# A decoder trunk on one core: the side products of the attention stage moved to other places in the order of work

## What is computed

```python
h = rmsnorm(x, g_attn)
(q_a, kv_cmp, kv_slc, kv_win, gate_a, q_b, k_b, v_b, r_b, lr_b, merge) = split(h @ w_in)
# attention: three branches, each softmax(q k^T - slope * distance) v
kv_c = compress_kv(concat(past_cmp, kv_cmp))         # 16-row blocks, small MLP
o_cmp, p_cmp = cmp_attend(q, kv_c)                   # over the compressed blocks
idx = top-16 blocks by p_cmp                         # 64 rows each
o_slc = sel_attend(q, blocks[idx])                   # over the selected rows
o_win = win_attend(q, last 512 rows)                 # over the recent rows
o_a = ga0 * o_cmp + ga1 * o_slc + ga2 * o_win
# gated linear attention from q_b, k_b, v_b, lr_b; swish gate r_b  -> o_b
mix = sigmoid(merge_a) * (o_a @ w_pa) + sigmoid(merge_b) * (o_b @ w_pb)
x = x + mix @ w_out
x = x + (gelu(causal_dwconv3(h2 @ w_u)) * (h2 @ w_g)) @ w_down,   h2 = rmsnorm(x)
```

## Time and profile before

| | |
|---|---|
| median of 3 runs | 2435.87 us (2433.31 to 2438.61) |
| profiled execution | 2436.56 us, span 2434.8 us |
| PE busy | 2385.6 us (98%), 13063 matmul instructions |
| DVE, ACT, POOL busy | 809.5, 539.0, 104.8 us |
| mean granted clock of PE | 0.986 of 2.4 GHz |
| attention stage, layer 0 | about 100 to 515 us of the span |
| attention stage, layer 1 | about 1306 to 1720 us of the span |

### The profile page before, as it was taken

One profiled execution on the slowest core, in us unless ns is written; L12 is line 12 of the kernel. 1 busy time (PEld: TensorE's weight loads), 2 busy tenths in 40 slices (PEclk: granted clock), 3 DMA queues, 4 the chain that ended last, 5 costly groups with the idle time before them and its releaser, 6 DMA issues.

```text
span 2434.8 us, 30974 instructions
## 1 busy us (share of the span) xinstructions
PE 2385.6 (98%) x13063; PEld 1926.0 (79%) x13063; DVE 809.5 (33%) x1893; ACT 539.0 (22%) x1085; POOL 104.8 (4%) x190
## 2 busy tenths in 40 slices
PE   8999899999999999999999999999999999999999
PEld 7787766678888888888888877667788888888887
DVE  4554545544114222210035544465441232222000
ACT  2353124432011111110013522244220111111000
POOL 4010010001000000000000100000000000000000
PEclk9999999999999999999999999999899999999999
DMA  7553421112222222212373544111122222222222
GB/s 231 186 200 142 197 95 52 32 41 89 70 72 70 70 78 79 66 51 72 77 265 130 219 162 183 53 36 36 49 95 72 69 70 70 70 82 65 63 72 73
DMA packets 186988, 237.55 MB, mean 98 GB/s; under 512 B 38047, under 2 KB 172704, under 8 KB 181984
## 3 DMA queue, kind: packets, MB, share of 16 engines
q1 hardware_dynamic: 175208, 133.11, 18.4%
q0 software_dynamic: 11200, 102.36, 11.1%
q10 hardware_dynamic: 444, 0.12, 0.0%
HBM read 222.76 MB, written 21.11 MB: 100 GB/s over the span
## 4 chain that ended last, share of the span: by engine, by line
PE 93%; DVE 4%; DMA 1%; ACT 1%; issue 1%; SPq 0%; POOL 0%; DVEq 0%; ACTq 0%; POOLq 0%
PE PS L818 52%; PE PS L1441 13%; PE PS L840 6%; PE PS L938 4%; PE PS L866 2%; DVE arena L1810 2%; PE PS L926 2%; PE PS L437 2%; PE PS L1219 2%; PE PS L1208 2%; PE PS L1136 1%; DMA arena<-in_cache_kv_slc_dram,idx 1%; ACT arena L1472 1%; PE PS L1181 1%; PE PS L1147 1%
## 5 line engine op out<-in xcount | busy, mean ns | idle before, releaser
L818 PE MATMUL PS<-hT,ring 128*128 128x272 f32 x4352 | 1010.1, 394 | 2.5 <-DVE small L2254 1.9
L818 PEld LDWEIGHTS PS<-hT,ring 128*128 128x128 f32 x4352 | 827.9, 191 | 175.5 <-issue 8.7
L1472 ACT ACTIVATE arena<-PS 64x512 f32<-64x512 f32 (+13 forms) x467 | 231.3, 518 | 1185.8 <-PE PS L818 559.8
L1441 PE MATMUL PS<-arena,ring 128*128 128x272 f32 x1408 | 323.7, 393 | 0.0
L1441 PEld LDWEIGHTS PS<-arena,ring 128*128 128x128 f32 x1408 | 268.0, 191 | 54.1
L1810 DVE COPY arena<-PS 64x512 f32<-64x512 f32 (+4 forms) x201 | 142.7, 710 | 268.6 <-PE PS L818 98.4
L1801 DVE TENSOR_TENSOR arena<-PS,arena 128x544 f32<-128x544 f32 (+3 forms) x124 | 76.0, 624 | 398.2 <-PE PS L818 380.9
L818 PE MATMUL PS<-arena,ring 128*128 128x272 f32 x768 | 177.2, 393 | 3.1 <-DVE arena L1801 3.1
L818 PEld LDWEIGHTS PS<-arena,ring 128*128 128x128 f32 x768 | 146.2, 191 | 33.5 <-DVE arena L1801 4.0
L1807 DVE SCALAR_TENSOR_TENSOR arena<-arena,prm 128x32 f32<-128x32 f32 (+1 forms) x176 | 88.1, 500 | 249.1 <-ACT arena L1472 245.8
L1801 DVE TENSOR_TENSOR xT<-PS,xT 128x544 f32<-128x544 f32 x32 | 23.2, 724 | 386.3 <-PE PS L1441 303.2
(11 more groups left out here) (309 smaller groups left out, 1665.3 us busy)
## 6 DMA issues: line engine op xcount, KB each, us to landing
ring<-in_w_up_dram SPq DMA_DIRECT2D x88, 512.0 KB, 4.6
ring<-in_w_in_dram SPq DMA_DIRECT2D x68, 512.0 KB, 4.8
ring<-in_w_down_dram SPq DMA_DIRECT2D x32, 384.0 KB, 3.8
ring<-in_w_down_dram SPq DMA_DIRECT2D x32, 320.0 KB, 4.5
arena<-in_state_kv_win_dram POOLq DMA_DIRECT2D x4, 2048.0 KB, 20.4
ring<-in_w_out_dram SPq DMA_DIRECT2D x16, 512.0 KB, 4.1
out_dram<-in_state_kv_win_dram POOLq DMA_DIRECT2D x2, 4064.0 KB, 23.8
ring<-in_w_in_dram SPq DMA_DIRECT2D x16, 256.0 KB, 5.0
```

Source lines behind the costliest of these rows:

```text
L818: mm = pe.matmul(PS[0:m, b + a, 0:HALF], weight(k), rhs(k)[:, HALF * a:HALF * a + HALF], start=(k == 0), stop=(k == nk - 1))
L1441: mm = pe.matmul(PS[:, b + a, 0:HALF], w[:, k, :], aT[:, 11 * half + k, HALF * a:HALF * a + HALF], start=(half == 0 and k == 0), stop=(hal ...
L1472: return nc.scalar.activation(out, in_, func, **kw)
```

## The change

The side products move to other places. No product is added or removed, and no arithmetic changes.

| place | before | after |
|---|---|---|
| behind `hidden(33)`, new ("s",0,5) | none | vb00 |
| ("s",0,4) | vb0l (two tiles) | vb01 |
| ("s",0,3) | qb0 | qb0 |
| ("s",0,2) | qb1 | qb1, kb0 |
| ("s",0,0) | kb0 | kb1 |
| ("b",0) | kb1, vb0b | vb0b, vb0h |
| ("b",1) | vb0h | vb1l |
| ("b",2) | vb1l | vb1h, vb1b |
| ("s",1,0) | vb1h, vb1b | rb00, in pool "S", copied once `os1` is filled |
| ("u",0) | rb00 | rb01 |
| ("u",j) | 11 products at 2,5,8,11,14,17,20,23,25,28,31 | 10 products at 2,5,8,11,14,17,20,23,26,30 |

Besides, `ost` with its wait for `os_ready` moves behind `vbf`, `score(0)` and `score(1)` on PE, and its copies on DVE behind `maxima(0)` and `maxima(1)`. ACT no longer takes `exps(2)` ahead of its copies of unit 0.

```diff
@@ -198,9 +198,9 @@
...
-    at = {("s", 0, 4): ("vb0l",), ("s", 0, 3): ("qb0",), ("s", 0, 2): ("qb1",), ("s", 0, 0): ("kb0",), ("b", 0): ("kb1", "vb0b"),
-          ("b", 1): ("vb0h",), ("b", 2): ("vb1l",), ("s", 1, 0): ("vb1h", "vb1b"), ("u", 0): ("rb00",)}
-    for j, name in zip((2, 5, 8, 11, 14, 17, 20, 23, 25, 28, 31), ["rb01", "rb10", "rb11"] + [f"ga{m}" for m in range(KC)]):
+    at = {("s", 0, 5): ("vb00",), ("s", 0, 4): ("vb01",), ("s", 0, 3): ("qb0",), ("s", 0, 2): ("qb1", "kb0"), ("s", 0, 0): ("kb1",),
+          ("b", 0): ("vb0b", "vb0h"), ("b", 1): ("vb1l",), ("b", 2): ("vb1h", "vb1b"), ("s", 1, 0): ("rb00",), ("u", 0): ("rb01",)}
+    for j, name in zip((2, 5, 8, 11, 14, 17, 20, 23, 26, 30), ["rb10", "rb11"] + [f"ga{m}" for m in range(KC)]):
         at["u", j] = (name,)
@@ -953,6 +953,20 @@
...
+                def side(place, pool="T"):
+                    for name in SIDE_AT.get(place, ()):
+                        s = wload(f"ma{int(name[2:]) // 2}" if name[:2] == "ga" else name[:-1])
+                        if name[:2] == "vb":
+                            if name[3] == "b":
+                                few(name, s, 256)
+                            else:
+                                tm(name, s, 0, 256, 256, {"0": (0,), "1": (1,), "l": (0, 1), "h": (2, 3)}[name[3]])
+                        elif name[:2] == "ga":
+                            fm(pool, name, s, P * (int(name[2:]) % 2))
+                        else:
+                            fm(pool, name, s, P * int(name[-1]))
                 turn(0)
@@ -975,22 +989,10 @@
...
                     hidden(j)
+                    if j == 33:
+                        side(("s", 0, 5))
                     if j % 4 == 2 and j > 4:
                         compressed(j // 4 - 1)
-                def side(place, pool="T"):
-                    for name in SIDE_AT.get(place, ()):
-                        s = wload(f"ma{int(name[2:]) // 2}" if name[:2] == "ga" else name[:-1])
-                        if name[:2] == "vb":
-                            if name[3] == "b":
-                                few(name, s, 256)
-                            else:
-                                tm(name, s, 0, 256, 256, {"l": (0, 1), "h": (2, 3)}[name[3]])
-                        elif name[:2] == "ga":
-                            fm(pool, name, s, P * (int(name[2:]) % 2))
-                        else:
-                            fm(pool, name, s, P * int(name[-1]))
                 side(("s", 0, 4))
@@ -1159,7 +1161,7 @@
...
                         block_scores(0)
-                    side(("s", hf, 0))
+                    side(("s", hf, 0), "TS"[hf])
                     pe.wait_ge(*S.at(pe, "es", hf + 3))
@@ -1186,13 +1188,6 @@
...
-                pe.wait_ge(*S.at(pe, "os_ready", 1))
-                pe.wait_ge(*S.claim(pe, "T", "ost"))
-                b = S.banks(pe, "ost")
-                pe.nop().then_inc(*S.inc(pe, "settled"))
-                for hf in range(2):
-                    mm = pe.transpose(PS[0:HD, b + hf, 0:P], oS[:, hf, :], ident[:, :])
-                mm.then_inc(*S.fill(pe, "ost"))
                 pe.wait_ge(*S.claim(pe, "T", "vbf"))
@@ -1238,10 +1233,17 @@
...
                 score(1)
+                pe.wait_ge(*S.at(pe, "os_ready", 1))
+                pe.wait_ge(*S.claim(pe, "T", "ost"))
+                b = S.banks(pe, "ost")
+                pe.nop().then_inc(*S.inc(pe, "settled"))
+                for hf in range(2):
+                    mm = pe.transpose(PS[0:HD, b + hf, 0:P], oS[:, hf, :], ident[:, :])
+                mm.then_inc(*S.fill(pe, "ost"))
                 side(("u", 0))
...
                 score(3)
-                for name in ("vbf", *SIDE_AT["u", 0]):
+                for name in ("ost", *SIDE_AT["u", 0]):
                     pe.wait_ge(*S.drained(pe, name))
@@ -1691,7 +1693,7 @@
...
                 for j, (qt, r, br) in enumerate(units):
-                    ahead = j + 3 if j == 0 or ("u", j - 1) in SIDE_AT else j + 2
+                    ahead = j + 3 if ("u", j - 1) in SIDE_AT else j + 2
                     while done < min(ahead, len(units)):
@@ -1994,12 +1996,6 @@
...
-                for j in range(36):
-                    if j % 2 == 1:
-                        turned_piece(dv, copy, j)
-                    if j % 4 == 1 and j > 4:
-                        hid_add(j // 4 - 1)
-                hid_add(8)
                 def side_copy(place):
@@ -2011,14 +2007,22 @@
...
                             else:
-                                t0 = {"l": 0, "h": 2}[name[3]]
-                                move = copy(vT[:, t0:t0 + 2, cc], PS[:, b, :].rearrange("p (t n) -> p t n", t=2))
+                                t0, t1 = {"0": (0, 1), "1": (1, 2), "l": (0, 2), "h": (2, 4)}[name[3]]
+                                move = copy(vT[:, t0:t1, cc], PS[:, b, 0:256 * (t1 - t0)].rearrange("p (t n) -> p t n", n=256))
                         else:
...
+                for j in range(36):
+                    if j % 2 == 1:
+                        turned_piece(dv, copy, j)
+                    if j == 33:
+                        side_copy(("s", 0, 5))
+                    if j % 4 == 1 and j > 4:
+                        hid_add(j // 4 - 1)
+                hid_add(8)
                 side_copy(("s", 0, 4))
@@ -2215,25 +2219,18 @@
...
                         block_softmax(0)
-                    side_copy(("s", hf, 0))
+                        side_copy(("s", hf, 0))
                     dv.wait_ge(*S.filled(dv, f"pt{hf}1"))
...
                     dv.wait_ge(*S.filled(dv, f"os{hf}"))
+                    if hf:
+                        side_copy(("s", hf, 0))
                     b = S.banks(dv, f"os{hf}")
...
                 dv.nop().then_inc(*S.inc(dv, "os_ready"))
-                dv.wait_ge(*S.filled(dv, "ost"))
-                b = S.banks(dv, "ost")
-                for g in range(G):
-                    for hf in range(2):
-                        v = PS[0:HD, b + hf, 0:P].rearrange("p (b g r t) -> p g r b t", b=4, g=G, r=R)
-                        last = copy(oST[HD * g:HD * g + HD, :, 16 * hf:16 * hf + 16].rearrange("p r (b t) -> p r b t", t=TS), v[:, g])
-                last.then_inc(*S.drain(dv, "ost"))
-                dv.wait_ge(*S.drained(dv, "ost"))
-                dv.nop().then_inc(*S.inc(dv, "arena_gla"))
                 dv.wait_ge(*S.filled(dv, "vbf"))
@@ -2320,6 +2317,15 @@
...
                 maxima(1)
+                dv.wait_ge(*S.filled(dv, "ost"))
+                b = S.banks(dv, "ost")
+                for g in range(G):
+                    for hf in range(2):
+                        v = PS[0:HD, b + hf, 0:P].rearrange("p (b g r t) -> p g r b t", b=4, g=G, r=R)
+                        last = copy(oST[HD * g:HD * g + HD, :, 16 * hf:16 * hf + 16].rearrange("p r (b t) -> p r b t", t=TS), v[:, g])
+                last.then_inc(*S.drain(dv, "ost"))
+                dv.wait_ge(*S.drained(dv, "ost"))
+                dv.nop().then_inc(*S.inc(dv, "arena_gla"))
                 weigh(0)
```

## The result

The changed kernel takes 2414.17 us (median of 4 runs, 2411.85 to 2416.12) beside 2437.01 us before (4 runs); the ratio is 0.9907, with a 95% interval of 0.9895 to 0.9919. The gain is 22.8 us, where 17.6 were forecast (2418.3 us); the time is inside the range.

A forecast was written before the change was run, and what follows sets the result against it. PE, busy 98% of the span, bounds the kernel, so gains come only from its waits and half clock. 13.0 + 4.0 + 1.0 + 0.8 - 1.2 = 17.6 us, median about 2418.3 us, range 2411 to 2427.

The forecast's parts named there:

- (b): Half 0's key turning: kb0 ahead of it covers the gather wait; gain 13.0 us, range 10 to 13.5.
- gathers later: Rival: gathers land later because vb1's weights share the engines; 2427 us if 3 us come back per layer; chance 0.1.
- the slower case: Rival: half 1's gathers collide with ring loads; slower from 12 us delay per layer, 2440 us at 14; chance 0.03.
- (a): End of key pieces: vb00 between thin pieces leaves one shorter clock fall; gain 4.0 us, range -1.2 to 8.2.
- as before: Rival: the clock falls for as long, same place or later; (a) is -1.2, total 2423.5 us; chance 0.22.
- never: Rival: the clock doesn't fall in the key stage; (a) is 8.2, total 2414 us; chance 0.13.
- (c): Before the unit loop: `vbf` and scores ahead of `ost` fill the `os_ready` wait; gain 0.5 us per layer, 1.0 together.
- (d): Unit 1's turn: moving ACT's `exps(2)` removes a 0.86 us wait; gain 0.4 us per layer, 0.8 together.
- (e): Units 27 to 30: PE waits at unit 30 for DVE's weights; loss 0.6 us per layer, 1.2 together.

The follow-up runs named there:

- The shifted table alone: Kernel before with only the products' new places (kb0 ahead of the key turning, later ones a place earlier); split, `ost` and exps moves undone: 2426.98 us, ratio 0.9962.
- the bare wait: Changed kernel, ACT's new order kept, with PE made to wait at unit 1's turn for the exponentials of unit 2: 2423.22 us, ratio 0.9937.
- the three together: Changed kernel plus `hid_add(7)` ahead of vb00's copy, fourth mixer product between up3 and up4, last unit product behind unit 29: 2403.89 us, ratio 0.9861.
- the moved mixer product: Changed kernel with the fourth mixer product placed between up3 and up4 of linear attention instead of ahead of them: 2409.68 us, ratio 0.9889.

## Why the prediction was right, and where it was off

**(b), the gather: right.** 13.0 forecast, 13.4 in the trace. Neither "gathers later" nor the slower case came: `turn_k(1)` starts 29.98 instead of 29.48 us after the first `block_turn` of layer 0, as 0.6 us more side work says, and waits for no gather. The shifted table alone gave 9.3 us. Of the 4 us between, the table's own costs explain 2.1 (0.6 and 0.45 us per layer, both traced). The rest is within the interval of that run, 3.4 us either side.

**(a), the split: right in size, partly by luck.** Forecast 4.0; the timings say 3.2 alone and 3.9 inside the change. The changed kernel's own profile shows 8.4, and I first took that for the value: the theory that the clock simply never falls. It did not hold. In the nine profiled kernels that have the split, the clock fell at this place in 5 of 18 layer passes, always in layer 1, for 3.4 to 6.8 us; in the four that have vb0l behind the last piece it fell in 8 of 8, for 6.8 to 10.2. So it is neither the rival "as before" nor "never", but something rarer and shorter. The forecast took one shorter fall in every layer, over vb01; no layer 0 had one, and of the five in layer 1 only two lay there (the split alone, and the old exps order), right behind the wait of 0.36 us at `compressed(7)`. The other three (`ost` put back, the bare wait, the three together) began inside `hidden(33)`, ahead of vb00, and lay over vb00. There the rival's argument held, that the thin work ahead of vb00 may bring the fall by itself; but the fall lasted only 3.4 us there. By these counts the stage alone gains about 3.2 us per layer: mean half clock 8.5 us before, worth 4.3; 1.3 us after, worth 0.7; and 0.37 us of wait. That is 6.4 us for both, more than the timings' middle values. In the profile with the split alone some 3 us were given back in the unit loop, which would close the gap. That is argued and not shown, since it is one profile, and that one 2.5 us above its median. Inside the full change, where that place is quiet, the gap between 3.9 and 6.4 stays open; the intervals of the two kernels are too wide to say that it is one.

**(c), `ost`: the term was 0.5 us per layer, traced 0.47.** But the sum did not say what the old place would cost in the new order. There it is 1.2 us per layer, and in one layer 1.6 us of half clock on top. The wait that moved to `score(1)` is 0.47 us, under the 0.8 that the forecast allowed.

**(d), ACT's exps: the mis-sized term.** The prediction counted the wait of 0.86 us, let 0.3 us of it come back at unit 2, and took 0.4 us per layer, "bounds 0 and 0.86 each". Traced it is 2.5 us per layer, outside these bounds: 0.9 of wait, since nothing came back at unit 2, and 1.6 of half clock, which the term put at nothing. By timing it is 5.6 us for both layers alone and 7.8 inside the change. The clock's fall behind it, 3.4 us from 357.5 on, stood in the trace of before (it is in the 0.94 of that stretch) and was not connected with the wait ahead of it. With (d) at 5.6 instead of 0.8 the sum is 22.4, and the measured gain is 22.8. The timed parts say the same without the forecast: 9.3 for the table, 3.2 for the split, 5.6 for the exps and 4.1 for `ost` are 22.2. Each has an interval of 2 to 3.5 us either side, so that both come so close is partly luck.

On (a) the Trainium skill's rule ("TensorE: Matmul & The Clock Gate", "HAM oscillation") was weighed in the prediction. It speaks of gaps in which PE waits for a transfer. The bare wait agrees with it in part, with 0.78 us of idle time on ACT rather than on a transfer. The key pieces disagree: with vb0l unsplit the clock falls there while PE is busy for 18.00 of 18.00 us.

**(e): right in place, 0.45 instead of 0.6 us per layer,** and a second wait in reach of the last product was overlooked, that at the turned output. It is no cost of the change, since the kernel before has it as well, with the product behind unit 31:

```profile
PE PS L1269 <- DVE arena L1810: 1.1, 2, 0.5
```

But it could be had with the other: behind unit 29 both go, 1.17 us per layer.

**What stayed as forecast.** The half clock of the late stages stays, in two places per layer: 6.8 and 6.8 us in layer 0 and 3.4 and 10.2 in layer 1 before, 6.8 and 6.8, 6.8 and 10.2 after. How long changes from one profile to the next, so a single profile is good to some 3 us here.

**Not settled:** why only layer 1 still falls at the key pieces, when a wait brings half clock and when it does not (0.8 to 0.9 us at unit 1 did it in 9 of 10 passes, 2.02 us at `os_ready` in one of four), whether the place of the dense work or the longer wait brought the fall with both tiles behind `hidden(33)`, and whether a part of the split's gain is lost again inside the full change.

## What to carry to other kernels

Don't count a wait of PE in thin work (many small matmuls) at its length only: here 0.8 us before a row of small matmuls cost 3.7 us per layer, while 2 us at another place cost its length in three passes of four. List where the granted clock falls, look at what PE did ahead of each place, and put a dense product between thin parts there, or take the wait away. The first gave 3 to 4 us although it removed no idle time, the second three times the idle time it removed. And judge such a change by runs, since one profile can flatter: the one here is 2.3 us under its median, and read alone it gave 8.4 us for a part that the runs put at 3 to 4.

## What was not expected of the hardware

- A wait of 0.78 us, added among matmuls of 128 columns, was followed by half clock for 6.8 us (a mean of 0.72 over 12 us); the same order of work without it had 1.00.
- A wait of 2.02 us in the same place of both layers was followed by 1.00 in one and 0.79 over 8 us in the other, and in another kernel by 1.00 in both.
- In one order of work the fall at the key pieces came in some passes and not in others, 5 of 18. Three of the five began with no wait ahead of them, two right behind one of 0.36 us that the passes without a fall mostly had as well.
- Where a fall was prevented, a later one was sometimes longer: 10.2 instead of 6.8 us in the stage behind the moved mixer product, and 6.8 instead of 3.4 us in the unit loop of the kernel with the split alone. That the one brings the other isn't shown.
